# Long convolutions: summing two residues on TensorE in two of eight units of input spectra

## The reference, cut to what matters

```python
def fftconv(u, k, bias):
    L = u.shape[1]
    U = jnp.fft.rfft(u, n=2 * L, axis=1)
    K = jnp.fft.rfft(k, axis=0)
    y = jnp.fft.irfft(U * K[None], n=2 * L, axis=1)[:, :L]
    return y + u * bias.astype(jnp.float32)
...
        z = v.astype(f32)
        for n, gate in enumerate((x1, x2)):
            k = bidir_kernel(filt[:, n, 0], filt[:, n, 1])
            z = gate.astype(f32) * fftconv(z, k, filt_bias[l, n])
```

## Time and profile before

| | us |
|---|---|
| median of three runs | 3959.01 (3958.61 to 3959.4) |
| the profiled execution's own time | 3965.33 |
| its span, first to last instruction | 3963.4 |
| mean granted clock of TensorE | 0.969 of full |
| the stage of the change | about 2224 to 2590 of the span |

### The profile page before, as it was taken

How to read it: one execution, slowest core, us unless ns; L and a number is a source line. 1 busy time by engine, 2 the same in 40 slices (tenths; PEclk the granted TensorE clock), 3 DMA queues, 4 the chain that set the end, 5 groups by cost and what they waited for, 6 DMA issues and landing times. The chain is left out here.

```text
span 3963.4 us, 42184 instructions
## 1 busy us (share of the span) xinstructions
PE 3711.4 (94%) x16780; PEld 2853.8 (72%) x16780; DVE 2842.3 (72%) x2581; ACT 1856.4 (47%) x1719; POOL 260.6 (7%) x281
## 2 busy tenths in 40 slices
PE   8989989799999799999999987899499999999998
PEld 3557766688888677777887533577288888888886
DVE  2645445889898675655346699954698888998887
ACT  3243431687877334443011111210277777777776
POOL 0000000100000200000000000000000101010110
PEclk9999999899999899999999998999799999999999
DMA  3003024899999632223344533143599999999998
GB/s 118 6 11 116 22 71 159 321 417 415 417 415 353 228 126 72 67 67 103 95 122 143 201 142 102 53 159 120 192 369 387 383 389 379 390 381 389 388 383 319
DMA packets 367168, 891.04 MB, mean 225 GB/s; under 512 B 21994, under 2 KB 118609, under 8 KB 357556
## 3 DMA queue, kind: packets, MB, share of 16 engines
q1 hardware_dynamic: 323796, 758.12, 51.5%
q0 software_dynamic: 26896, 97.17, 7.0%
q10 hardware_dynamic: 16336, 33.82, 2.2%
HBM read 788.65 MB, written 100.40 MB: 224 GB/s over the span
## 5 line engine op out<-in xcount | busy, mean ns | idle before, releaser
L2342 DVE TENSOR_TENSOR moe_w_rest<-moe_w_w,moe_upper 128x2048 fp32r<-128x2048 f32 x384 | 862.2, 2287 | 134.5 <-ACT moe_upper L2243 68.5
L2243 ACT ACTIVATE moe_upper<-moe_w_w 128x2048 fp32r<-128x2048 f32 x192 | 357.4, 1909 | 233.3 <-PE moe_y_ps L2207 87.2
L2342 DVE TENSOR_TENSOR moe_w_rest<-moe_w_w,moe_upper_w 128x2048 fp32r<-128x2048 f32 x192 | 430.4, 2282 | 14.5 <-ACT moe_upper_w L2261 14.3
L2261 ACT ACTIVATE moe_upper_w<-moe_w_w 128x2048 fp32r<-128x2048 f32 x192 | 357.5, 1910 | 117.3 <-PE moe_up_ps L2181 72.5
L2251 ACT ACTIVATE moe_upper<-moe_w_w 128x2048 fp32r<-128x2048 f32 x192 | 356.7, 1912 | 3.5 <-DMA moe_w_w<-in_w_up_dram 3.5
L2181 PE MATMUL moe_up_ps<-moe_upper,moe_x_upper 128*128 128x512 f32 x768 | 308.6, 402 | 0.0
L2181 PE MATMUL moe_gate_ps<-moe_upper,moe_x_upper 128*128 128x512 f32 x768 | 300.8, 392 | 4.7 <-DVE moe_x_rest L2355 4.7
L2181 PE MATMUL moe_gate_ps<-moe_upper,moe_x_rest 128*128 128x512 f32 x768 | 300.4, 391 | 0.0
L2181 PE MATMUL moe_gate_ps<-moe_w_rest,moe_x_upper 128*128 128x512 f32 x768 | 300.1, 391 | 0.0
L2181 PE MATMUL moe_up_ps<-moe_upper,moe_x_rest 128*128 128x512 f32 x768 | 300.1, 391 | 0.0
L2181 PE MATMUL moe_up_ps<-moe_w_rest,moe_x_upper 128*128 128x512 f32 x768 | 299.0, 389 | 0.0
(11 more groups left out here) (623 smaller groups left out, 7517.2 us busy)
## 6 DMA issues: line engine op xcount, KB each, us to landing
moe_w_w<-in_expert_w_dram SPq DMA_DIRECT2D x96, 2048.0 KB, 11.1
moe_w_w<-in_w_gate_dram SPq DMA_DIRECT2D x64, 2048.0 KB, 11.7
moe_w_w<-in_w_up_dram SPq DMA_DIRECT2D x64, 2048.0 KB, 11.0
moe_w_w<-in_w_down_dram SPq DMA_DIRECT2D x64, 2048.0 KB, 10.9
tmp_y_rows<-moe_y ACTq DMA_DIRECT2D x32, 512.0 KB, 9.4
block_w_first<-in_w_in_dram SPq DMA_DIRECT2D x20, 512.0 KB, 3.8
tmp_h<-out_xn POOLq DMA_DIRECT2D x16, 512.0 KB, 3.0
tmp_spectra<-held_K ACTq DMA_DIRECT2D x8, 1024.0 KB, 4.8
```

Source lines behind the costliest of these rows:

```text
L2243: act.activation(half(upper1(c), h), half(weights.w1[c % 2], h), ACT.Copy).then_inc(m.w1_rounded, 1)
L2261: act.activation(half(upper2(i, c), h), half(weights.w2[c % 2], h), ACT.Copy).then_inc(m.w2_rounded, 1)
L2342: dve.tensor_tensor(half(rest, h), half(whole, h), half(upper, h).bitcast(F32), ALU.subtract).then_inc(done, 1)
```

## The change

In the units (0,1) and (2,0), slots 0 and 2 become sums on TensorE: slot 0 accumulates the spectra of the residues of slots 0 and 1 in PSUM, slot 2 those of slots 2 and 3, each with eight float32 matmuls instead of four. Slots 1 and 3 stay as they are. VectorE's first addition, which made these two sums, falls away in these two units; its next step is unchanged. The waits for chunks move: slot 0 waits for the chunks of slots 0 and 1, slot 2 for those of slots 2 and 3, and slots 1 and 3 for none. The requests on SyncE are unchanged.

```diff
+    SUMMED = ((0, 1), (2, 0))
...
         def input_spectra(n, fh):
+            summed = (n, fh) in SUMMED
+            loaded = -1
             for i in SLOTS:
-                v = RADIX * (HF * n + fh) + i
-                r = RESIDUE[i]
-                chunk = u[v % N_CHUNKS]
-                pe.wait_ge(u_loaded[v % N_CHUNKS], 16 * (v // N_CHUNKS + 1))
-                spectrum(place["U", n, fh] + i, fh, ([(COS_OF[r], 0, r)], [(SIN_OF[r], 0, r)]), lambda part, r, j: chunk[:, j, :])
+                of = (i, i + 1) if summed and i % 2 == 0 else (i,)
+                chunks = {}
+                for at in of:
+                    v = RADIX * (HF * n + fh) + at
+                    chunks[RESIDUE[at]] = u[v % N_CHUNKS]
+                    if at > loaded:
+                        pe.wait_ge(u_loaded[v % N_CHUNKS], 16 * (v // N_CHUNKS + 1))
+                        loaded = at
+                terms = ([(COS_OF[r], 0, r) for r in chunks], [(SIN_OF[r], 0, r) for r in chunks])
+                spectrum(place["U", n, fh] + i, fh, terms, lambda part, r, j: chunks[r][:, j, :])
...
             dve.wait_ge(fwd_copied, u_made(n, fh))
-            add(x[:, 0:3:2], x[:, 1:4:2])
+            if (n, fh) not in SUMMED:
+                add(x[:, 0:3:2], x[:, 1:4:2])
             back_to(0)
```

## The result

| | before | changed |
|---|---|---|
| median of ten runs, us | 3958.81 (3952.79 to 3964.52) | 3966.28 (3959.65 to 3972.53) |
| ratio | | 1.0018, 95% interval 1.001 to 1.0026 |
| profiled execution: time, span | 3965.33, 3963.4 | 3966.63, 3965.0 |
| L: first copy of U(0,0) to the start of I(1) | 170.54 | 176.68 |
| first product of pass 1 | 176.26 | 182.92 |

The change costs 7.5 us by the medians; the interval of the ratio is 4 to 10 us, and its middle is 0.18%, just under the 0.2% that I had taken as the bound. The two profiled spans differ by only 1.6 us, because one execution of this kernel differs from the next by several microseconds (the ten runs of the kernel before span 12 us), and part of that lies ahead of this stage: in the changed kernel's profile the stage begins 4.3 us earlier (the first copy at 2223.86 us instead of 2228.20 us).

What follows compares the result with a forecast made beforehand. VectorE was taken to bound the stage's middle, with TensorE only 3.2 us ahead at pass 0's first product. Shift +5.9, lead -3.2, pace +1.8, (2,0) 0 gave +4.4 us: 3963.4 us, range 3956.5 to 3968 us.

Steps and rivals of the forecast that it cites:

- the sum as worked out: Whole kernel: the terms add to +4.4 us, ending between 3961.5 and 3966 us; chance 0.65.
- Slot 0: First summed slot of unit (0,1): 3.74 us after a stop plus 3.43 us for the extra matmuls, from start to copy.
- Chunk 3's landing and slot 2: Unit (0,1): chunk 3 lands 3.9 us after its request, so TensorE stands about half a microsecond before slot 2.
- The long wait: Rival, slot 2 of unit (0,1): chunk 3 lands up to 9.6 us after request, ending at +10.1 us; chance 0.09.
- The stop ahead of U(1,0) goes: TensorE's 2.84 us chunk wait before unit (1,0) vanishes, its chunk landing 9.6 us after request, now ahead of need.
- TensorE's shift at I(0): TensorE's start on the banks for pass 0's products: 5.9 us later, at 2318.0 us.
- r0: VectorE's first of eight products with results in a pass; in pass 0 predicted 2.7 us late.
- The pace: VectorE's eight products of pass 0 follow TensorE at 3.43 us a bank for the first six, adding 1.8 us.
- (2,0) hidden on both sides: Unit (2,0): TensorE's extra 6.9 us falls into 30.60 us idle, VectorE's saved addition into a wait; gain nothing.
- I(1) starts cold as before: TensorE's banks for pass 1's products: after some 20 us idle still at 1.2 GHz; warm, 2 us would return.
- Nothing takes the loss up behind: Behind the convolutions no slack takes up the 4.4 us; the rival that it is taken up later had chance 0.14.
- The saving survives: Rival, units (0,1) and (2,0): VectorE gains 2.3 us, or 2.3 us more, ending at 3956.7 to 3954.4 us; chance 0.12.

Runs made afterwards that it cites:

- fill_before: Changed kernel plus four matmuls with overwritten result behind U(0,0), ahead of TensorE's wait for the chunks of U(0,1); L 175.57 us, one time of 3969.0 us.
- s20_only: Changed kernel with only U(2,0) summed, U(0,1) as before; ratio to the kernel before 0.9994 (0.9985 to 1.0004), L 170.57 us.
- add_kept: Changed kernel with VectorE's two additions kept, so the output is another; L 176.46 us, no ratio given.
- s01_only: Changed kernel with only U(0,1) summed, U(2,0) as before; ratio to the kernel before 1.0018 (1.0008 to 1.0027), L 176.43 us.
- warm_fill: Changed kernel plus two matmuls with overwritten result between the two chunk waits of slot 0 of U(0,1); L 177.81 us, no ratio given.
- k_behind: Changed kernel with pass 0's two stored filter spectra requested behind the next unit's first two chunks; ratio to the kernel before 1.0007 (0.9998 to 1.0016), L 172.40 us.
- no_add: Changed kernel with the two additions left out and nothing summed on TensorE, so the output is another; L 169.95 us, no ratio given.
- none_summed: Changed kernel's code with an empty list of summed units, the same work as the kernel before; L 170.56 us, no ratio given.
- late_wait: Changed kernel with the wait for a summed slot's second chunk moved to the first matmul reading it; ratio to the kernel before 1.0009 (1.0 to 1.0018).
- warm_only: Kernel with no unit summed, only 22 and 18 matmuls with overwritten result in two TensorE idle times; ratio to the kernel before 0.9985 (0.9976 to 0.9994).
- s31_only: Changed kernel with only the last unit, U(3,1), summed instead; ratio to the kernel before 0.9992 (0.9983 to 1.0001).
- s31_warm: Only U(3,1) summed, plus 22 and 18 matmuls with overwritten result in two TensorE idle times; ratio to the kernel before 0.9978 (0.9968 to 0.9987).

## Why the prediction was right, and where it was too small

The times: forecast +4.4 us, 3963.4 us, range 3956.5 to 3968.0 us; measured 3966.28 us. Right in direction and within the range, though 0.3 us above the 3961.5 to 3966 us that I had given to the sum as worked out. By size the loss was underestimated, 4.4 us against 6.1 to 6.9 us in the stage and 7.5 us in the medians. The mechanism (TensorE's shift less its lead, then its pace, and nothing from (2,0)) came out as written; one term of the sum was too small.

- *U(0,1)'s chunk and the start of the unit*: predicted 13.4 us after the first copy (2241.6 - 2228.20), measured 2237.34 - 2223.86 = 13.48 us. Right.
- *Slot 0*: predicted 3.74 + 3.43 = 7.17 us from start to copy, measured 22.32 - 13.48 = 8.84 us. **This is the term that was mis-sized**: the 1.67 us are the clock's, shown by fill_before (1.69 us). The fault lies in the step that took the cost of a start after a stop from the slot after the 1.76 us stop and used it for a stop that I had myself lengthened by 1.4 us. In the fourteen profiles the stops ahead of U(0,1) after which the clock fell are the longer ones (2.60 to 3.25 us, against 1.52 to 2.37 us where it stayed up), so the change made the fall likelier at this place without being its only cause. I had looked at the clock only at I(1), where the idle time was long.
- *Chunk 3's landing and slot 2*: predicted 3.9 us and a stop of half a microsecond; measured 3.8 us and 0.46 us. The long wait, the rival on the slower side, did not come.
- *The stop ahead of U(1,0) goes*: right, chunk 0 of U(1,0) landed 6.6 us after its request, not 9.6 us, and there was time to spare:

```profile
hytab_u<-tmp_v_x SPq DMA_DIRECT2D x1, 512.0 KB, 3.8
...
hytab_u<-tmp_v_x SPq DMA_DIRECT2D x1, 512.0 KB, 6.6
```

- *TensorE's shift at I(0)*: predicted 5.9 us, measured 91.49 - 83.90 = 7.6 us, the difference being slot 0 again. *r0*: predicted 2.7 us late, measured 4.4 us.
- *The pace*: predicted 25.53 us from r0 to r7, measured 25.53 us. Right to the hundredth, because pass 1 of the kernel before showed the case.
- *(2,0) hidden on both sides*: right, by s20_only and add_kept. The idle time before I(1) shrank to 22 us, predicted some 20 us.
- *I(1) starts cold as before*: it did, but the clock came back later: 6.24 us instead of 5.72 us from the start of I(1) to the first product, 0.5 us of the 6.7 us. s20_only had 5.64 us and s01_only 6.27 us at the same place, warm_fill 5.70 us and k_behind 6.66 us, so this half microsecond is not tied to the change by any run here.
- *Nothing takes the loss up behind*: M says 6.9 us, the medians 7.5 us. Right within what they resolve. In the one profile 1.5 us do come back behind M: the last product of I(3) is 5.4 us late (368.25 us after the first copy against 362.90 us), because in I(3)'s second half the clock came back after two groups of matmuls where it took four before. Its rows before and after:

```profile
2591.10 1.09 DVE L4442 TENSOR_TENSOR merge_z<-hyena_inv_ps,merge_z 128x512 f32<-128x512 f32 x1 [1.23 <-PE hyena_inv_ps L4372]
...
2592.11 1.09 DVE L4450 TENSOR_TENSOR merge_z<-hyena_inv_ps,merge_z 128x512 f32<-128x512 f32 x1 [1.21 <-PE hyena_inv_ps L4380]
```

- *The saving survives*: it fell. no_add shows that it was worth 0.6 us at I(1) and, with a later clock, 0.1 us at pass 1's first product, so my -2.3 us for that case was too high as well; I had the pace in the main sum but not in the rival.

Two things stay open. I(3) has a stop of 2.7 to 3.9 us ahead of its third bank, and M is some 3 us longer in most of the profiles in which the clock fell there. The stretches of 2 us in which that bank begins, first of s01_only, then of the kernel before:

```profile
2561.29:2563.29 2.00, 1.97 (x5) 1.61 (x6) 1.97 (x2) 0.00 (x0) 0.00 (x0) 0.50 0.04 8
```

```profile
2558.20:2560.20 2.00, 2.00 (x10) 1.76 (x10) 1.97 (x3) 0.00 (x0) 0.00 (x0) 1.00 0.00 0
```

It stayed up in before, none_summed, changed, s20_only, add_kept and warm_fill, after stops of 3.2 to 3.5 us, and fell in s01_only, late_wait, k_behind, fill_before and warm_only, after stops of 2.7 to 3.1 us, and late in no_add, after 3.9 us. A longer stop is thus not what makes it fall here. The five that fell at once have the shorter stops because TensorE had run longer at the low level in the two banks ahead: the mean granted clock over the 12.58 us from the start of I(3) to that bank was 0.77 in all five, 0.82 to 0.85 in the six that stayed up, and 0.88 in no_add. Nothing in the edits explains the split. If the change makes the fall more frequent, that would be a part of its 7.5 us that one profile can't show; the runs do not decide it. And the gap between 6.9 us at M, or 5.4 us at the last product, and 7.5 us in the medians is within the interval.

## What to carry to other kernels

When an engine is back to back, that does not yet make its work worth removing: look for the next point at which it takes something from another engine, and count by how much that other is ahead there. Work moved onto that other engine must fit into its lead, and behind the meeting point the pair runs at the pace of the slower for as long as results are passed one by one. Before summing on TensorE, look for the unit that ends in TensorE's idle time; of the units tried, the last one gained 2.6 us in the stage (in time its interval just reaches no change), the one ahead of a long idle time was free, and the one inside TensorE's gapless stretch lost 6 us.

## What the runs showed of the hardware that I had not expected

The granted clock fell to the 1.2 GHz level after quite short stops of TensorE inside a busy stage. Ahead of U(0,1) it fell in all six profiles with a stop of 2.60 to 3.25 us (s31_only, warm_fill, add_kept, s01_only, changed, s20_only) and stayed at 1.00 in all six with a stop of 1.52 to 2.37 us (none_summed, no_add, warm_only, before, late_wait, s31_warm). Yet the length alone does not decide it. Ahead of U(1,0) it fell after 2.27 us in no_add and stayed up after 2.84 us in before and 3.38 us in warm_only. The same 32 records take 15.58 us in the first of these rows (no_add) and 14.00 us in the second (warm_only):

```profile
2250.50 15.58 PE L4329 MATMUL hyena_fwd_ps<-hytab_u,hytab_tr 128*128 128x512 f32 x32 [2.27 <-DMA hytab_u<-tmp_v_x]
...
2251.10 14.00 PE L4329 MATMUL hyena_fwd_ps<-hytab_u,hytab_tr 128*128 128x512 f32 x32 [3.38 <-DMA hytab_u<-tmp_v_x]
```

In I(3) it fell after some stops of 2.7 to 3.1 us and stayed after others of 3.2 to 3.5 us. One such fall costs 1.6 to 1.7 us in a slot of matmuls of 512 columns, summed or not. The Trainium skill, TensorE: Matmul & The Clock Gate, section "What's actually happening", says that "the default state is throttled, and activity releases the throttle"; the runs agree, and useless matmuls are such an activity: 22 of them ahead of I(1) cost VectorE nothing and returned 1.9 us at its first product (174.39 us against 176.26 us).
